# Attention mixers of a two-block model: the values matmuls moved in front of the scores, the outputs of value groups taken one step sooner

## What is computed

```
proj = h @ w_in;  a, b, c, d = split(proj)
o_a = window attention  (4 heads; band of 3 key blocks, distance bias, a sink logit)
o_b = latent attention  (4 heads; q and kv from normed low-rank latents, rotary)
o_c = axial attention   (4 heads; q and k normed and rotated, dense keys)
o_d = diff attention    (4 heads; softmax(q1 k1) - lam * softmax(q2 k2), then a norm)
return concat(o_a, o_b, o_c, o_d) @ w_out
# each softmax: s = q @ k.T * scale (+ bias);  p = exp(s - max) / sum;  o = p @ v
```

## Time and profile before

| | |
|---|---|
| median of 3 runs | 3512.36 us (3507.78 to 3513.71) |
| the profiled execution | 3510.07 us, its span 3508.3 us |
| TensorE busy | 3367.8 us, 96% of the span |
| VectorE / ScalarE busy | 1803.3 us (51%) / 1411.4 us (40%) |
| mean DMA rate | 82 GB/s |
| chain that ended last | TensorE 84%, VectorE 9%, ScalarE 4%, issue 3%, DMA 1% |

### The profile page before, as it was taken

One profiled execution on the slowest core, in us unless ns is written; L12 is line 12 of the kernel. 1 busy time (PEld: TensorE's weight loads), 2 busy tenths in 40 slices (PEclk: granted clock), 3 DMA queues, 4 the chain that ended last, 5 costly groups with the idle time before them and its releaser, 6 DMA issues.

```text
span 3508.3 us, 47079 instructions
## 1 busy us (share of the span) xinstructions
PE 3367.8 (96%) x17468; PEld 2774.4 (79%) x17468; DVE 1803.3 (51%) x2572; ACT 1411.4 (40%) x2167; POOL 12.7 (0%) x13
## 2 busy tenths in 40 slices
PE   7999999999999999999998999999999999899997
PEld 6898888888788888888865778888888866588886
DVE  5573566537766534333577553335333576563335
ACT  5323344326544324222456442224232457542223
POOL 0000000001000000000000000000000000000000
PEclk9999999999999999999999999999999999999998
DMA  3201232322232322222211122222223210122233
GB/s 130 67 31 37 80 102 96 99 95 93 76 102 96 99 95 95 97 97 95 76 43 35 43 78 96 98 97 89 96 96 99 80 52 28 35 76 96 96 98 102
DMA packets 89736, 288.48 MB, mean 82 GB/s; under 512 B 9968, under 2 KB 14576, under 8 KB 89072
## 3 DMA queue, kind: packets, MB, share of 16 engines
q1 hardware_dynamic: 89440, 284.69, 24.6%
q0 software_dynamic: 144, 1.71, 0.1%
HBM read 284.26 MB, written 2.10 MB: 82 GB/s over the span
## 4 chain that ended last, share of the span: by engine, by line
PE 84%; DVE 9%; ACT 4%; issue 3%; DMA 1%; DVEq 0%; ACTq 0%; SPq 0%
PE gb L583 24%; PE gb L584 24%; PE gb L585 24%; PE gb L1244 2%; DVE wl L2023 1%; PE pm L1257 1%; PE pm L1277 1%; DVE rinv L2053 1%; ACT wh L1405 1%; ACT h L1455 1%; DMA wst<-in_weights 1%; DVE h L2039 1%; DVE work_a L2656 1%; ACT work_a L1893 1%; ACT xh L1467 0%
## 5 line engine op out<-in xcount | busy, mean ns | idle before, releaser
L583 PE MATMUL gb<-xh,wh 128*128 128x512 f32 (+1 forms) x3168 | 1193.7, 377 | 59.7 <-DVE xl L2077 31.6
L584 PE MATMUL gb<-xl,wh 128*128 128x512 f32 (+1 forms) x3168 | 1169.9, 369 | 0.0
L585 PE MATMUL gb<-xh,wl 128*128 128x512 f32 (+1 forms) x3168 | 1169.8, 369 | 0.0
L2023 DVE TENSOR_TENSOR wl<-wst,wh 128x1024 fp32r<-128x1024 f32 (+3 forms) x600 | 646.5, 1091 | 447.3 <-ACT wh L1405 441.2
L1405 ACT CAST wh<-wst 128x1024 fp32r<-128x1024 f32 (+3 forms) x600 | 555.7, 942 | 604.4 <-DMA wst<-in_weights 604.2
L583 PEld LDWEIGHTS gb<-xh,wh 128*128 128x128 f32 x3168 | 605.7, 191 | 197.4 <-issue 49.9
L584 PEld LDWEIGHTS gb<-xl,wh 128*128 128x128 f32 x3168 | 607.2, 192 | 99.1 <-issue 4.9
L585 PEld LDWEIGHTS gb<-xh,wl 128*128 128x128 f32 x3168 | 606.6, 191 | 98.6
L583 PE MATMUL gb<-hid,wh 128*128 128x512 f32 (+2 forms) x1276 | 471.6, 370 | 10.3 <-DVE wl L2023 9.5
L585 PE MATMUL gb<-hid,wl 128*128 128x512 f32 (+2 forms) x1276 | 467.9, 367 | 0.0
L584 PE MATMUL gb<-hid,wh 128*128 128x512 f32 (+2 forms) x1276 | 467.8, 367 | 0.0
(11 more groups left out here) (401 smaller groups left out, 2989.9 us busy)
## 6 DMA issues: line engine op xcount, KB each, us to landing
wst<-in_weights SPq DMA_DIRECT2D x408, 512.0 KB, 3.3
wst<-in_weights SPq DMA_DIRECT2D x84, 384.0 KB, 3.0
wst<-in_weights SPq DMA_DIRECT2D x84, 320.0 KB, 2.9
h<-in_x_t SPq DMA_DIRECT2D x2, 1024.0 KB, 6.1
out_t<-h SPq DMA_DIRECT2D x8, 256.0 KB, 2.3
tab<-in_first SPq DMA_DIRECT2D x1, 1984.0 KB, 14.9
wst<-in_weights SPq DMA_DIRECT2D x20, 96.0 KB, 2.1
tab<-in_second POOLq DMA_DIRECT2D x1, 1666.0 KB, 7.3
```

The source lines that it names most:

```text
L583: pe.matmul(dst, w_hi, x_hi, start=start, stop=False)
L584: pe.matmul(dst, w_hi, x_lo, start=False, stop=False)
L585: return pe.matmul(dst, w_lo, x_hi, start=False, stop=stop)
L2023: dve.tensor_tensor(wl[:, s, m, a], wst[:, s, m, a], f32(wh[:, s, m, a]), ALU.subtract).then_inc(lo_split, 1)
```

## The change

In a mixer's steps 5 to 39, `values` of the step four back are issued directly before `scores(u)`, not behind the second half of the projections. From step 40 on the order stays. `take(y)`, `high_y(y)` and `low_y(y)` with y of 3 and more stand one step sooner in the programs of ScalarE and VectorE: the steps of `Y_STEP` become 11, 19, 23, 27, 31, 35, 39, 43 where they were 12, 20, 24, 28, 32, 36, 40, 44. No instruction is added or removed.

```diff
-Y_STEP = {LAST[4 * y_ + 3] + 5: y_ for y_ in range(8)}
+Y_STEP = {LAST[4 * y_ + 3] + 4: y_ for y_ in range(8)}
...
                         for c, i in projected[:ahead]:
                             part_of(c, i)
+                        if u - 4 in LAST:
+                            values(LAST.index(u - 4))
                         scores(u)
                         for c, i in projected[ahead:]:
                             part_of(c, i)
                     else:
                         for k in ((0, 1), (2, 3), (4, 5), (6,))[u - NS]:
                             out_part(k)
-                    if u - 4 in LAST:
+                    if u >= NS and u - 4 in LAST:
                         values(LAST.index(u - 4))
                     if u - 2 in LAST:
                         turn(LAST.index(u - 2))
```

## The result

The changed kernel takes 3525.51 us in the median of 11 runs (3516.86 to 3527.95), the kernel before 3509.89 us in 11 runs (3507.78 to 3513.71). The ratio is 1.004, with a 95% interval of 1.0032 to 1.0049: slower by 15.6 us, twice what a measurement of this kernel can tell from no change. The forecast was 3515.8, its upper bound 3525.0. The profiled execution of after took 3526.1 us.

The account below looks back on a forecast made before the run. TensorE, busy 96% of the span, can gain only where it waits for chains of VectorE and ScalarE. Terms -0.4 + 0.5 + 0 + 1.0 + 0.9 - 0.3 = +1.7 per mixer, +3.4 on 3512.4: 3515.8 us, range 3504 to 3525.

Parts of the forecast that it names:

- same: Whole kernel: time not told apart from before, within about 0.2% or 7 us; chance 0.71.
- +1.7 for a mixer: Sum of all step terms in one mixer: 1.7 us slower, +3.4 for both mixers.
- -0.3 for steps 29 to 35: Steps 29 to 35 of a mixer: 0.9 us gained, 0.6 lost at the turn of step 33, net 0.3 us faster.
- nothing from step 36 on: From step 36 of a mixer on: TensorE has no gap, so the order changes nothing.
- the wait at `scores(9)`: Step 9 of a mixer: the wait of 1.85 us falls to about 0.8, and the values there take 1.0.
- `swap(3)`: Idle time in front of it grows from 1.16 to about 3.5 us, with a take ahead of the third root.
- `scores(24)`: Step 24 of a mixer: starts 1.1 us later, and its wait stays within 0.4 of what it was.
- the projection of chunk 12: Its wait for the weight remainder, 4.2 us before, grows by about 1.
- -0.4, +0.5, +1.0, +0.9: Terms in us for one mixer, loss as plus: steps 9 to 12, 13 to 16, 25, 26 to 28, in that order.
- the turn of step 31: Its idle time grows to some 3.5 us, one of three longer waits in the slower rival about the clock.
- Rival 1: Each value fills a wait in front of its scores for good: 6.4 us gained per mixer, 3500 in all; chance 0.12.
- Rival 2: Three longer waits each bring a lower-clock stretch, mean 0.93 or less: 4.2 us per mixer, 3524 in all; chance 0.2.

Follow-up runs that it names:

- experiment 3: Kernel before with values moved in front of scores only in steps 9, 11, 23, 24, 30 and 32, takes at their old step: 3537.26 us.
- Experiment 6: Changed kernel with high_y(3) and low_y(3) back in step 28, the take itself still in step 27: 3522.89 us.
- experiment 2: Kernel before with only the takes one step sooner (Y_STEP + 4), TensorE's order as before: 3529.2 us.
- experiment 7: Kernel before with both edits only from step 33 on (takes 5 and later sooner): 3517.74 us.
- experiment 10: Kernel before with both edits only in steps 5 to 19 (takes of groups 0 and 1 sooner): 3510.02 us.
- Experiments 8: Kernel before, neither edit, with the split of weight chunk 12 moved from the end of step 27 to that of step 26: 3504.84 us.
- experiment 12: Changed kernel with the split of weight chunk 12 moved from step 27 to step 26: 3511.29 us.
- experiment 9: Changed kernel with both edits undone from step 33 on: 3521.71 us.
- experiment 11: Kernel before, neither edit, with the splits of chunks 12, 14 and 15 moved from steps 27, 30, 32 to 26, 34, 37: 3494.35 us.
- experiment 1: Kernel before with values in front of scores as in the change, takes at their old step: 3540.03 us.

## Where the prediction was right and where it was wrong

It was wrong in its likeliest case, "same": the kernel is slower by 0.4%, 9.7 us above the number and 0.5 above the range. The direction of the sum was right, its size was not: +1.7 for a mixer came as 5.4 and 7.7 in the profile. Two steps of it failed: the end of the sum, which had -0.3 for steps 29 to 35 and nothing from step 36 on, and the clock, which it took as unchanged.

**Right: that idle time moves and is not filled.** Nearly every place named beforehand came out: the wait at `scores(9)` 0.96 (about 0.8 said); `swap(3)` 3.48 (about 3.5) with the take in front of the root; `scores(24)` 1.1 later, of which its own values are 1.0, so the sum's 0.1 is left (its wait fell by 0.4, as allowed, that of `scores(23)` to 0.5, by more than I had said, and `turn` got two new waits there, 0.35 in front of `scores(24)` and 0.29 behind it); `scores(16)` 0.3 later; the projection of chunk 12 started 1.9 later where the terms up to it (-0.4, +0.5, +1.0, +0.9) make 2.0; the turn of step 31 3.66 (3.5). At `scores(34)` the first mixer is 2.2 us late, 1.4 less its own values, where the sum says 1.7. Rival 1, the waits filled, is out: the waits in front of `scores` fell by 3.6 us, and TensorE's idle time in all rose by 6.0. Even the wait at step 9, where 1.4 us were gained at first, gave nothing in the end (experiment 3).

**Right in time, wrong in place: chunk 12.** Its projection starts as late as I had said, but the wait there is 4.29, about as before (4.2), and not 1 longer. Experiment 6 shows the 0.9 of `high_y(3)` in it (4.3 against 3.4). The rest had gone into a wait that I did not have, 0.7 at the `turn` before it (step 27), and the timeline of ScalarE in after shows where it comes from:

```profile
1903.92 0.59 ACT L1907 COPY work_a<-pm 128x512 f32<-128x512 f32 x1 [0.50 <-PE pm L1277]
1904.40 0.59 ACT L1882 COPY work_a<-pm 128x512 f32<-128x512 f32 x1
```

The take, one step sooner, waits for the values of the same step, and the `copy_turned` for `turn` is queued behind it: experiment 2's wait in small.

**Wrong: "From step 36 on TensorE has no gap, and the order changes nothing."** The prediction itself says that the move loses 1.03 us where a chain ends at a `turn` behind the scores, because the values that covered it are gone. It did not apply this to the last steps, where no wait was shown. The room there could be read off before (timeline of ScalarE, then of TensorE, in step 38):

```profile
1955.67 1.01 ACT L1880 COPY work_a<-pm 128x1024 f32<-128x1024 f32 x1
1957.76 1.09 PE L1257 MATMUL pm<-com,work_a 128*128 128x128 f32 x8
```

The `copy_turned` ends at 1956.68. A `turn` that waits for one starts 0.14 us behind its end, as in the chain of waits above (1942.61 to 1942.74). This one could thus have started at 1956.82, and its room is 0.94 us, less than the 1.03 of the values in front of it. Once they are gone, it waits. In after, steps 37 and 38:

```profile
1959.02 1.98 PE L1244 MATMUL gb<-work_a 96*128 96x512 f32 x4
1960.84 1.04 PE L1257 MATMUL pm<-com,work_a 128*128 128x128 f32 x8
...
1962.83 1.98 PE L1244 MATMUL gb<-work_a 96*128 96x512 f32 x4
1963.64 1.01 ACT L1882 COPY work_a<-pm 128x1024 f32<-128x1024 f32 x1
1964.79 1.06 PE L1257 MATMUL pm<-com,work_a 128*128 128x128 f32 x8
```

In step 37 `turn` starts 1.82 us behind `scores`, as `values` did in before (1.81): there is no wait. In step 38 it starts 1.96 behind, and 0.14 behind the end of the copy (1964.65): it waited 0.14, which the bracket doesn't show because the ends of matmuls are modelled. By this measure, what lies over 1.82, `turn` waits 0.38, 0.25, 0, 0.14 and 0.46 in steps 35 to 39 of experiment 7, where before has no such wait. That makes 1.2 us, about all that the first mixer of its profile loses from step 33 on. In after the first mixer loses 5.0 from step 33 on. Such waits make 1.3 of it in steps 36 to 39, the longer wait at the `turn` of step 33 makes 0.9 (2.07 for 1.22), and 2.0 fall in step 34 at the lower clock.

**Wrong: the clock left out of the sum.** Rival 2 had it, with a chance of 0.2 and the time 3524, near the 3525.5 that came. But its mechanism, too, was only half right, so that its number came so near is luck. The idle time in front of `swap(3)`, its first place, cost nothing net (experiment 10). Its condition, a mean clock of 0.93 or less, holds in the profiled second mixer (0.93, 7.7 us longer) and not in the first (0.95, 5.4 us longer). In the first, the delay grows by 4.0 us from `scores(34)` (1.4, its values apart) to the end (5.4), and half of this, 2.0, falls in step 34: 3.78 us for 1.98 and 1.91 for 1.06, behind the wait of 2.07. In the second, steps 28 and 29 ran at the lower clock: at `scores(30)` it is 4.8 late, where the first is 1.1 late with the same order of work. What I hadn't seen is how it feeds itself: matmuls at the lower clock start a chain later, the chain of the other engines keeps its length, and wherever TensorE recovers sooner it waits longer at the chain's end, behind which the clock falls again. The profiles agree with this at one place, the `turn` of step 33: in all 28 mixers of the 14 kernels `scores(34)` ran at the full clock where that wait was 1.64 us or less, and partly or wholly at the lower one where it was 1.84 or more. Experiments 8 and 12 bear on this: with the wait for chunk 12 gone, which in before stands ahead of 8 us at the lower clock, the change costs 6.5 us instead of 15.6, although the waits of 3.5 at `swap(3)` and of 3.66 at step 31 are still there. So by the medians more than half of the cost needed the longest wait and what follows it; the uncertainty given with experiment 12 holds for this too.

**Not settled.** Of the 11 us of steps 20 to 32, experiment 9's profile has 10.4 in the middle third (3.1 and 7.3 us in the two mixers): 2.5 idle time, the other 7.9 longer matmuls. But one profile is one execution: after's own runs lie 11 us apart, and its two mixers, with the same instructions, differ by 2.4 us. The stretch that differs most is `scores(28)` to `scores(30)`, behind the wait for chunk 12. It takes 9.3 us (mean clock 1.00) in one mixer of after and 12.1 (0.64) in the other, 12.0 (0.65) and 15.1 (0.50) in experiment 9, 10.9 (1.00) and 15.3 (0.56) in experiment 11, each pair with the same instructions. The split between idle time and clock in the median run stays open, and so does what makes the clock fall at one wait and not at another of the same length.

## What to carry to other kernels

Moving independent work in front of a waiting instruction gains only if the chain that ends in this wait does not begin at an instruction that the same move delays; follow each chain to its start and to the wait after the next before counting the wait as room, and look for what else the moved work waits for (here the read of its output bank, which made the second edit necessary). Where the chains of the other engines set the waits, take work off them instead: three weight splits put at other steps gave 16.3 us where the reordering cost 15.6. And where waits of 2 to 4 us already come with a lower clock, price a longer wait with the clock behind it, and expect that price to vary from nothing to about as much again: the wait of 2.34 us at `swap(3)` in experiment 1 cost nothing more in one mixer and 2.1 us in the other.

## What the runs showed of the hardware

- The same instructions behind the same idle time ran at different clocks. In experiment 1 `swap(3)` waits 2.34 us in both mixers; from `scores(11)` to `scores(12)` it is 8.5 us in the first, at a granted clock of 1.00, and 10.6 in the second, at 0.78. In after the wait is 3.48 and 3.46 us, the clock falls in both, and the stretch takes 10.2 and 11.8 us. The moment of the fall differs: in the first mixer at 1804.1, some 2 us after TensorE had resumed, as the projection's matmuls of 256 columns show (0.28 us each up to the one at 1803.86, 0.41 to 0.42 from 1804.10 on); in the second about 2892.9, while it still waited, so that `swap(3)` itself took 1.88 us for 1.01. The Trainium skill ("TensorE: Matmul & The Clock Gate", A second HAM failure mode) tells of short idles between groups of matmuls that send the clock down and up; the rows agree in kind, and experiment 1 shows that the same idle does not always do it.
- Behind 2.07 us of idle time `scores(34)` took 3.78 us, behind 0.60 us 1.98. The shorter wait came here from slower matmuls ahead of it, so a shorter wait isn't by itself a sign of time gained.
- A wait of TensorE of 0.14 us can be missing from the waits view. `scores` of 96 rows takes 1.81 us to the next piece behind it in before and 1.82 in after; where a `turn` came 1.96 behind, ScalarE's copy had ended 0.14 before it, as in front of every `turn` with a wait that is shown.
